# Filler products and a new order in the opening of a hybrid trunk kernel, gate rows at two borders, and the high-weight products of the experts first

## What is computed

```python
def adaln(cvec, w, b):
    return jnp.split(jax.nn.silu(cvec) @ w + b, 6, axis=-1)

def sublayer(x, shift, scale, gate, g_pre, g_post, fn):
    h = rmsnorm(x, g_pre) * (1 + scale[:, None]) + shift[:, None]
    out, aux = fn(h)
    return x + gate[:, None] * rmsnorm(out, g_post), aux
```

```python
def swiglu(x, w1, w3, w2):
    return (jax.nn.silu(x @ w1) * (x @ w3)) @ w2

for e in range(N_EXPERTS):
    out = out + dense_gate[:, e:e + 1] * swiglu(t, w1[e], w3[e], w2[e])
```

## Time and profile before

| | before |
|---|---|
| median of 3 runs | 1476.66 us (1475.51 to 1476.97) |
| the profiled execution, its own time | 1477.1 us |
| its span in the trace | 1475.5 us |
| PE busy | 1366.9 us (93%) |
| VectorE busy, ScalarE busy | 878.7 us (60%), 749.4 us (51%) |
| moved by DMA | 358.17 MB, mean 243 GB/s |
| mean granted TensorE clock | 0.972 of full speed |

### The profile page before, as it was taken

How to read it: one execution, slowest core, us unless ns; L and a number is a source line. 1 busy time by engine, 2 the same in 40 slices (tenths; PEclk the granted TensorE clock), 3 DMA queues, 4 the chain that set the end, 5 groups by cost and what they waited for, 6 DMA issues and landing times.

```text
span 1475.5 us, 18785 instructions
## 1 busy us (share of the span) xinstructions
PE 1366.9 (93%) x7242; PEld 1074.6 (73%) x7242; DVE 878.7 (60%) x1203; ACT 749.4 (51%) x978; POOL 95.2 (6%) x170
## 2 busy tenths in 40 slices
PE   5899899899999997999878799999999996999996
PEld 1899456799998886888557687566877742888884
DVE  1533586623333436679576596555976602979796
ACT  2531476622223326497345485444866402768783
POOL 0221430000000000200000200000000000000002
PEclk7999999999999999999999899999999998999999
DMA  9743997733334233233680698657998799999994
GB/s 360 229 130 114 346 386 260 263 115 115 114 116 152 99 118 114 86 114 114 236 293 6 235 390 327 255 211 253 402 337 289 275 378 409 405 354 410 363 396 138
DMA packets 132219, 358.17 MB, mean 243 GB/s; under 512 B 6220, under 2 KB 30184, under 8 KB 132008
## 3 DMA queue, kind: packets, MB, share of 16 engines
q1 hardware_dynamic: 120048, 321.41, 59.5%
q0 software_dynamic: 9344, 32.25, 6.4%
q10 hardware_dynamic: 2744, 3.36, 0.7%
HBM read 335.34 MB, written 22.55 MB: 243 GB/s over the span
## 4 chain that ended last, share of the span: by engine, by line
PE 80%; DVE 9%; DMA 4%; ACT 4%; issue 1%; ACTq 0%; SPq 0%; DVEq 0%
PE bank L2206 31%; PE bank L1864 12%; PE bank L1643 7%; PE bank L1875 6%; PE bank L2156 6%; PE bank L1691 4%; PE bank L1640 3%; PE bank L1584 2%; DMA ring<-in_moe_w_dram 1%; DMA ring<-in_mod_w_dram 1%; DMA arena<-in_moe_w_dram 1%; DVE ring_parts L2339 1%; DVE arena L2638 1%; PE bank L1618 1%; PE bank L2096 1%
## 5 line engine op out<-in xcount | busy, mean ns | idle before, releaser
L2206 PE MATMUL bank<-arena_parts 128*128 128x512 f32 x1072 | 290.8, 395 | 10.1 <-DVE arena_parts L2985 10.1
L2878 DVE TENSOR_TENSOR ring_parts<-ring,arena_parts 128x2048 fp32r<-128x2048 f32 x85 | 192.5, 2286 | 97.1 <-ACT arena_parts L1407 53.6
L2206 PEld LDWEIGHTS bank<-arena_parts 128*128 128x128 f32 x1072 | 200.8, 190 | 61.1 <-issue 17.6
L1407 ACT ACTIVATE arena_parts<-ring 128x2048 fp32r<-128x2048 f32 x85 | 161.6, 1917 | 38.5 <-DMA ring<-in_moe_w_dram 30.4
L2206 PE MATMUL bank<-ring_parts,arena_parts 128*128 128x512 f32 x504 | 157.1, 393 | 0.0
L1864 PE MATMUL bank<-ht_parts,arena_parts 128*128 128x384 f32 x352 | 118.3, 336 | 0.2
L1864 PE MATMUL bank<-xn_parts,arena_parts 128*128 128x384 f32 x352 | 117.8, 335 | 0.0
L1864 PE MATMUL bank<-ht_parts,ring_parts 128*128 128x384 f32 x352 | 117.7, 334 | 0.0
L2206 PEld LDWEIGHTS bank<-ring_parts,arena_parts 128*128 128x128 f32 x504 | 95.8, 190 | 20.6
L2573 DVE TENSOR_TENSOR arena<-arena,bank 128x384 f32<-128x384 f32 x22 | 12.2, 554 | 125.4 <-PE bank L1864 125.4
L1643 PE MATMUL bank<-ht_parts,ring_parts 128*128 128x384 f32 x256 | 86.4, 338 | 0.0
(11 more groups left out here) (497 smaller groups left out, 2649.7 us busy)
## 6 DMA issues: line engine op xcount, KB each, us to landing
ring<-in_moe_w_dram SPq DMA_DIRECT2D x144, 1024.0 KB, 7.5
ring<-in_mod_w_dram SPq DMA_DIRECT2D x24, 2048.0 KB, 11.6
arena<-in_moe_w_dram SPq DMA_DIRECT2D x48, 1024.0 KB, 7.3
ring<-in_ff_w_dram SPq DMA_DIRECT2D x23, 1024.0 KB, 7.8
ring<-in_w_in_even_dram SPq DMA_DIRECT2D x6, 2048.0 KB, 11.5
ring<-in_w_in_odd_dram SPq DMA_DIRECT2D x6, 2048.0 KB, 8.0
ring<-in_ff_w_dram SPq DMA_DIRECT2D x5, 2048.0 KB, 7.8
routed<-cst POOLq DMA_DIRECT2D x1, 7168.0 KB, 23.6
```

The source lines that it names most:

```text
L1407: act.activation(whi_moe[high_at(w, n_)], e_half(j, h), ACT.Copy).then_inc(whi_ready, 1)
L2206: ins = pe.matmul(bank[base + b][:, :], lhs[:, c_, :], rhs[:, k, 512 * b:512 * b + 512], start=(first and h == 0 and k == 0 and n_ == 0), ...
L2878: dve.tensor_tensor(e_half(j, h, low=True), e_half(j, h), whi_moe[high_at(w, 2 * j + h)], ALU.subtract).then_inc(wlo_ready, 1)
```

## The change

There are four parts.

1. **Opening.** TensorE begins with four filler products (`keep_busy`: 128x512 in full float32, of a tile of zeros, into a bank that nobody reads) as soon as that tile is zeroed, and has six more behind the first turns, three behind `mod_turn(0)`, three behind `mod_turn(1)` and one behind `mod_turn(3)`. `mod_mm(2)` comes ahead of `mod_turn(1)` and `mod_mm(3)` ahead of `mod_turn(2)`. `mod_mm(2)` and `(3)` wait for ScalarE's copy of the bank (`mod_kept`) where they waited for VectorE's sum (`mod_added`).
2. **Gate rows at borders.** Sublayer 1's first gate row comes ahead of `turn_in(1, ...)`, its second one at f = 2. Both of sublayer 3's come ahead of `turn_in(3, ...)`; the second waits for `x_ready` 9, since it writes banks 4 and 5. ScalarE copies them behind `norm_tiles` and, for the last, behind the modulation. New waits on TensorE: `gb_kept` 3 ahead of the up products, `gb_kept` 7 ahead of the router's product, `gb_kept` 8 ahead of the first tokens' product.
3. **Tokens ahead of panels behind the small visit.** At j = 10 of a visit without a main tile, ScalarE's and VectorE's copies of the next visit's tokens come ahead of the splits of its first panel.
4. **High-weight products first.** For each half, `main_panel` does its eight products with the high weights as soon as `whi_ready` allows, and waits for `wlo_ready` only ahead of the last four. Before, it waited for `wlo_ready` at the start, with the low-weight products in the middle.

```diff
@@ -599,7 +599,7 @@
         def gate_bank(s, c_):
-            return {0: (4, 6), 1: (4, 4), 2: (4, 6), 3: (6, 6)}[s][c_]
+            return {0: (4, 6), 1: (6, 4), 2: (4, 6), 3: (6, 4)}[s][c_]
@@ -1198,6 +1198,7 @@
             norm_tiles(0)
+            keep_gate(1, 0)
@@ -1211,8 +1212,8 @@
                 act.activation(silt[:, f % 2, :], bank[6][:, 0:T], ACT.Silu).then_inc(silu_ready, 1)
-                if f in (3, 5):
-                    keep_gate(1, f // 5)
+                if f == 3:
+                    keep_gate(1, 1)
                 if f >= KF - F_RING:
@@ -1417,6 +1418,7 @@
             norm_tiles(2)
+            keep_gate(3, 0)
@@ -1426,6 +1428,7 @@
                 ins.then_inc(ht_act, 1)
+            keep_gate(3, 1)
@@ -1501,6 +1504,9 @@
                                .then_inc(og_ready, 1)
+                    if j == 10 and not main_of(w):
+                        for b in range(2):
+                            xg_hi(w + 1, b)
                     for h in range(2):
@@ -1509,8 +1515,6 @@
                         act.activation(sd[:, 0, j - 8:j - 7], epsc[:, :], ACT.Copy).then_inc(y_steps, 1)
-                    if isinstance(w, int) and w == 0 and j in (2, 4):
-                        keep_gate(3, j // 4)
                     if j in (1, 5) and main_of(w):
@@ -1526,7 +1530,7 @@
                                .then_inc(aeh_ready, 1)
-                    if j == 10 and not last and main_of(w + 1):
+                    if j == 10 and not last and main_of(w) and main_of(w + 1):
                         for b in range(2):
@@ -1575,8 +1579,10 @@
-                if m >= 2:
-                    pe.wait_ge(mod_added, m - 1 if m < 4 else m)
+                if m >= 4:
+                    pe.wait_ge(mod_added, m)
+                elif m >= 2:
+                    pe.wait_ge(mod_kept, m - 1)
                 i = panel(("mod", m))
@@ -1610,10 +1616,12 @@
-                if c_ and s in (1, 3):
-                    pe.wait_ge(gb_kept, 2 * s + 1)
-                elif c_ == 0:
+                if c_ == 0:
                     pe.wait_ge(gains_ready, s + 1)
+                    if s in (1, 3):
+                        pe.wait_ge(gb_kept, 2 * s)
+                elif s == 3:
+                    pe.wait_ge(x_ready, 9)
                 for k in range(KD):
@@ -1692,6 +1700,15 @@
+            blank = wgp[:, :, :, :].rearrange("p k g r -> p (k g r)")
+
+            def keep_busy(n):
+
+                for _ in range(n):
+                    pe.matmul(bank[3][:, :], blank[:, 0:P], blank[:, 0:512], start=True, stop=True)
+
+            pe.wait_ge(zeroed, 2)
+            keep_busy(4)
             pe.wait_ge(cst_in, 48)
@@ -1701,15 +1718,19 @@
             ins.then_inc(rows_turned, 1)
+            keep_busy(6)
             mod_mm(1)
             mod_turn(0)
+            keep_busy(3)
+            mod_mm(2)
             mod_turn(1)
-            mod_mm(2)
+            keep_busy(3)
+            mod_mm(3)
             mod_turn(2)
-            mod_mm(3)
             for k in range(2):
...
             mod_turn(3)
+            keep_busy(1)
             for k in range(2, 4):
@@ -1843,11 +1864,13 @@
+            gate_row(1, 0)
             for k in range(KD):
                 turn_in(1, k)
+            pe.wait_ge(gb_kept, 3)
             for f in range(KF):
-                if f in (2, 4):
-                    gate_row(1, f // 4)
+                if f == 2:
+                    gate_row(1, 1)
                 if f % 2 == 0:
@@ -2027,6 +2050,9 @@
+            pe.wait_ge(fin_kept, 1)
+            for c_ in range(CONDS):
+                gate_row(3, c_)
             for k in range(KD):
@@ -2041,6 +2067,7 @@
             pe.wait_ge(router_in, 32)
+            pe.wait_ge(gb_kept, 7)
             for k in range(KD):
@@ -2176,7 +2203,7 @@
                     if start:
-                        pe.wait_ge(gb_kept, 8)
+                        pe.wait_ge(route_ready, INDEXED)
                     else:
@@ -2196,12 +2223,14 @@
                         pe.wait_ge(ael_ready, mains(w) * 4 + (j - UP + 1))
-                    pe.wait_ge(wlo_ready, mains(w) * (2 * ITEM) + (KF + 2 * j + h + 1))
+                    pe.wait_ge(whi_ready, mains(w) * (2 * ITEM) + (KF + 2 * j + h + 1))
                     wh, wl = e_parts(w, j, h, 2)
-                    for k in range(2):
-                        c_ = 4 * (j - UP) + 2 * h + k if j >= UP else 4 * kk + 2 * h + k
-                        hi_, lo_ = (aeh, ael) if j >= UP else (xgh, xgl)
-                        for n_, (lhs, rhs) in enumerate(((hi_, wh), (hi_, wl), (lo_, wh))):
+                    hi_, lo_ = (aeh, ael) if j >= UP else (xgh, xgl)
+                    for n_, (lhs, rhs) in enumerate(((hi_, wh), (lo_, wh), (hi_, wl))):
+                        if n_ == 2:
+                            pe.wait_ge(wlo_ready, mains(w) * (2 * ITEM) + (KF + 2 * j + h + 1))
+                        for k in range(2):
+                            c_ = 4 * (j - UP) + 2 * h + k if j >= UP else 4 * kk + 2 * h + k
                             for b in range(2):
@@ -2234,10 +2263,6 @@
                             turn_act(w, (j - 4) // 4)
-                    if isinstance(w, int) and w == 0 and j in (1, 3):
-                        if j == 1:
-                            pe.wait_ge(route_ready, INDEXED)
-                        gate_row(3, j // 2)
                     if wide(w):
@@ -2257,6 +2282,7 @@
             pe.wait_ge(htok_ready, 6)
+            pe.wait_ge(gb_kept, 8)
             pe.wait_ge(route_ready, PICKED)
@@ -3042,6 +3068,9 @@
                         extra_product(w, (j - 4) // 4)
+                    if j == 10 and not main_of(w):
+                        for b in range(2):
+                            xg_lo(w + 1, b)
                     for h in range(2):
```

## The result

| | before | after |
|---|---|---|
| median of all runs on the same chip, us | 1476.44 (1475.46 to 1477.42, 7 runs) | 1469.07 (1462.49 to 1473.66, 7 runs) |
| ratio, 95% interval | | 0.9949 (0.9930 to 0.9968) |
| profiled execution, us (span) | 1477.1 (1475.5) | 1462.49 (1460.9) |
| mean granted clock of TensorE in it | 0.972 | 0.986 |

The kernel is faster by 7.5 us of 1476 by the ratio (4.7 to 10.3). Each step has to be read with that in mind.

What follows compares the result with a forecast made beforehand. TensorE, four fifths of the last-ending chain, was taken as the bound. Opening 4.6, border 1 2.1, border 3 1.2, visit 0 1.1 and small visit 2.1 sum to 11.1 us saved: 1465.6 us on the median's scale (1460.5 to 1471.5).

Steps and rivals of the forecast that it cites:

- The likeliest case: Whole kernel: all parts together save 11.1 us, giving 1465.6 us; chance 50%.
- The opening: Start up to the projection: fillers and reordering bring the first product to 37.3 from 41.16; 4.6 us with the clock.
- the opening gives little: Rival, opening: half clock during six fillers delays mod_mm(1), saving 1.9 us in place of 4.6; time 1468.5; chance 14%.
- Border 1: Border to sublayer 1: one gate row leaves the up products and goes into 6.00 us of idle time; 2.1 us.
- The 0.3 for a held clock: Border to sublayer 1: if the clock holds, the first turns come 0.3 us sooner.
- Border 3: Border to sublayer 3: gate rows break up 6.00 us of idle time, the clock should hold; 1.2 us (0.3 to 1.4).
- Visit 0: First visit of the experts: two gate rows leave TensorE's list, but VectorE bounds the next turn; 1.1 us of 4.0.
- The small visit: Behind the small visit: TensorE starts earlier, but loads and VectorE's product bound the turn; 2.1 us, stall some 3 us.
- The rule on transposes: Rival, opening and borders: transposes don't count as busy, so turns don't bring the clock up; time 1467.1; chance 12%.
- Splits don't bind: Rival: loads or VectorE have more slack, visit 0 gives up to 4.0 us, small visit about 5; about 1460; 11%.
- swallowed: Rival: a later wait or the clock's phase in routing swallows the gains; within 3 us of before; chance 8%.
- slower: Rival, opening: clock stays at 0.50 throughout, fillers take 1.80 us; 7.3 us slower, about 1484; chance 5%.

Runs made afterwards that it cites:

- e1_again: The changed kernel with no edit, in other executions: 1469.31 us.
- e3_gates: The kernel before with only the gate rows at the borders, with their copies and waits: 1472.92 us.
- e9_prod_first: The changed kernel with VectorE's product of the activations ahead of splits in visit 0 and the visit behind the small one: 1464.42 us.
- e7_warm: The changed kernel with filler products in seven idle gaps of TensorE: 1464.68 us.
- e6_high_only: The kernel before with only the high-weight products first, the tokens left behind the first splits: 1474.01 us.
- e2_opening: The kernel before with only the opening's part of the change: 1475.20 us.
- e8_no_fill: The changed kernel with all 17 filler products removed, everything else kept: 1471.75 us.

## Why the prediction was right, and where it was not

The forecast was 1465.6 (1460.5 to 1471.5), the measurement 1469.07, in the range and faster as forecast. The likeliest case gave 11.1 us, the kernel 7.5.

- **The opening: right mechanism, mis-sized term.** The step that failed is the sum's first: "Opening: 4.6 us". `mod_mm(1)` at 19.10 (forecast 18.99), `mod_mm(3)` at 1.92 us, fillers that fit: as forecast. The last panel was there at 30.04 and not at 29.0, so its product began 0.7 us later than forecast, and the first product of the projection came at 38.4 and not 37.3. Larger is the other end: 41.16 was read as the start of the projection in the kernel before, and it is one draw from 38.5 to 41.5. Measured: 1.3 us alone (0 to 2.7), 1.8 with the clock held. That miss of some 3 us is about the whole difference between 11.1 and 7.5. The rival "the opening gives little" named the right size with the wrong cause; no filler of the six ran at half clock.
- **Border 1: right.** 1.8 us from the row that left the up products. The 0.3 for a held clock did not come: 4.21 us of idle time were still followed by turns at half clock.
- **Border 3: right in range**, for 1.2: 1.6 us in the first trace of the changed kernel, 0.7 in e1_again and in e3_gates. In the first trace the turns ran at full clock, in e1_again partly not.
- **Visit 0: right bound and size, other source.** The turn waits for VectorE, as forecast, and e9_prod_first shows that VectorE's order is the cause. Beside the clock the trace has 0.9 us for 1.1. The forecast gave it to the gate rows that leave the visit. But high first with the gate rows still there makes 0.8 of it: 35.92 us to the turn, which then follows VectorE's product at once, against 35.79 in e7_warm, which has both edits and as much half clock there. The gate rows alone (e3_gates, 37.28 us against 36.70) settle nothing, as that stretch has 8.9 us at half clock where before has 3.4.
- **The small visit: right.** 2.1 to 2.2 us for 2.1 and a stall of 2.72 in front of the turn for about 3. Tokens first alone carries it; high first adds nothing there. "In all other visits the order changes nothing" was wrong for visit 0.
- **The rule on transposes** (the Trainium skill, TensorE: Matmul & The Clock Gate, Part 4: PE-mode transpose). In the changed kernel's trace 3.29 us of nothing but turns at border 3 ran at a clock of 1.00, and in e7_warm 2.96 at border 1. That no fall came there is weak evidence, as 3.13 us without any work left the clock at 1.00 too. Stronger is a rise at border 1 of the changed kernel: behind 4.21 us of idle time TensorE did nothing but turns from 276.95 to 281.98, at 0.50 throughout, and the next window of 1 us is

```profile
282.00:283.00 1.00, 1.00 (x7) 1.00 (x6) 0.79 (x3) 1.00 (x3) 0.00 (x0) 0.84 1.10 349
```

  (busy times, then clock, DMA share, GB/s). With the earlier trace rows that is a second place where turns came before the rise, and the traces don't agree with that rule for these float32 turns.
- **Splits don't bind, swallowed, slower: fell.** The first by e9_prod_first, the others by the ratio.
- **Slips in the sums.** "The opening gives little" comes to 1468.3 by its own terms, not 1468.5. The low ends named for the range (1468.5, border 3 at 0.3, visit 0 at nothing) add up to about 1470.5, not 1471.5, and its lower bound of 1460.5 leaves out the rival at 1460. The measurement lies inside either way.

The gain of 14.6 us between the two profiled executions is the sum of the steps and a difference in lost time (28.6 against 12.7 us). What remains open is why some executions lose the clock at a given gap and others not; no run here controls that.

## What to carry to other kernels

A saving of a few us is not to be measured against one trace of the kernel before where its clock stands at half: look whether the place comes out the same in other executions, and price it from their mean. Idle gaps like the ones filled here (3.1 to 6.75 us) in front of work that TensorE bounds are worth filling with products that write to a bank that is free, all along the kernel and not only at its start; five of them gave 5.6 us (3.5 to 7.5), the change's opening 1.3 (0 to 2.7). A gap whose next work only runs into another wait, like that of 2.10 us ahead of the pick of tokens, is not. And when a wait moves to another engine, look at what stands in front of the awaited instruction in that engine's list: moving VectorE's product past two splits in two visits was worth 2.7 and 1.6 us at the two turns in the traces.

## What the hardware showed that was not expected

- The same instructions behind the same idle time came out at either level: a gate row behind 1.87 us of idle took 2.05 us in one execution and 2.95 in the next, and the fourth modulation product took 3.20 us in the trace of before and 1.92 in that of e6_high_only, with nothing changed in front of it.
- A gap of 3.13 us ahead of the projection left the clock at 1.00 in the changed kernel's two traces. In e9_prod_first the same gap, behind the same instructions, was followed by four products at full speed and then by a fall:

```profile
39.00:42.00 3.00, 3.00 (x13) 2.90 (x12) 1.96 (x3) 0.42 (x1) 0.00 (x0) 0.51 1.05 384
```

  A gap of 3.74 us had it at 0.50 in e2_opening, and 2.92 us behind a warm product was enough in e8_no_fill. Length alone does not tell which comes.
- A filler can move half clock in place of removing it: in e7_warm the pick of tokens ran faster, and the clock fell behind it, in the first products of visit 0 (2.63 us for eight in place of 2.11).
